# One decoder layer on one core: attention worked in pairs of heads, and a step with another order

## The chip, the cores and the metric

The kernel runs on one core of a Trainium2 chip. The metric is the device time of one execution in microseconds (us); three executions of the kernel before gave 1241.56, 1243.33 and 1244.72 us, so the median is 1243.33 us.

## The reference

One layer of a decoder for 256 tokens of width 1024, all in float32. Cut to what matters here:

```
proj = rmsnorm(x) @ w_in            # 1024 -> 5120: q, k, v for two mixers, two gates
# mixer 1, 8 heads of 64: stick-breaking attention
log_keep = where(causal, -softplus(z), 0);  tail = reverse_cumsum(log_keep) - log_keep
a = where(causal, exp(log_sigmoid(z) + tail), 0);  y = a @ v
# mixer 2, 8 heads of 64: softmax attention with a relative bias
y = softmax(where(causal, z + bias, -inf)) @ v
h = x + (sigmoid(g1) * (y_sb @ w_proj_sb) + sigmoid(g2) * (y_mb @ w_proj_moba)) @ w_out
h = h + moe(rmsnorm(h))             # top 4 of 32 experts, each 1024 -> 2 x 1024 -> 1024
out = rmsnorm(h)
```

`z` is the product of queries and keys, scaled by 1/8. The weights of the 32 experts are 12 MB each.

## The kernel before

The order of the work on each engine is written out by hand, one queue per engine, with semaphores between them. TensorE (PE) does first the projection in "units" (`unit(u)`, L849): a unit is 8 matmuls over the 8 slices of the depth, into `bank[u % 2]`, and ScalarE (ACT) copies it out (`evacuate`, L467). A "T" unit gives 128 columns of q or k, transposed (128 by 256), an "N" unit gives a 128 by 512 tile of values or gates. Ten units run ahead of attention, 18 are left as fill: one in each of the 16 steps of attention (`fill_at`), and two more in steps 3 and 6 (`second_at`).

Attention goes head by head, heads 0 to 7 stick-breaking, 8 to 15 softmax (called MoBA in the names). Three pieces on PE belong to a head. `scores(s)` (L866) multiplies the head's 64 rows of q and k: even heads lie in partitions 0 to 63, odd ones in 64 to 127, so a head uses one half of the rows of the array. `middle(s)` (L886) is the cumulative sum by two triangle matrices for a stick-breaking head (full array), and three transposes of the probabilities for a softmax head. `mix_values(s)` (L903) multiplies 128 rows by the head's 64 columns of values, so it uses one half of the columns. A float32 matmul stands in the trace as two instructions, called passes below. A step of the loop at L922 is: scores of head s, fill unit, middle of head s-1, second unit if there is one, values of head s-2.

Between scores and middle of a stick-breaking head stand Abs, Exp and Ln on ACT (L490, L495, L496), max and add on VectorE (DVE, L659) and the causal mask on GpSimd (POOL, L407). Between middle and values stand Exp on ACT (L512) and the mask (L407). For a softmax head DVE adds the bias and takes the maxima, ACT does Exp (L502), DVE scales (L666 to L674), and after the transposes ACT copies (L515). DVE copies the output of a pair of heads to `yT` (L680).

After attention come the projections of the mixers (L945), the merge with the gates, `w_out` (L956), the router, and then the loop over the experts, which reads all their weights through a ring of 12 slots of 1 MB. SyncE (SP) issues the load of a slot when PE has used what lay in it (L310 gate and up weights, L315 down weights). The weights of the mixers' projection, of `w_out` and of the first expert go into the same ring, each load when the last unit of the columns that lay there is done.

Of the kernel before, what the change touches and what calls it, by code (L numbers as in the profile page):

```python
# [46 lines left out]
def hybrid_layer(nc, x, norm_mix_g, w_in, w_proj_sb, w_proj_moba, w_out, rel_bias, norm_ffn_g,  # L47
# [31 lines left out]
    for s in range(NH):  # L79
        fill_at[s] = len(units)  # L80
        units.append(first_fill[s])
        if s in second_fill:
            second_at[s] = len(units)
            units.append(second_fill[s])
# [8 lines left out]
    with ctx:  # L93
# [6 lines left out]
        bank = [ctx.enter_context(nc.psum_tensor(f"bank{i}", [P, 512], F32)) for i in range(8)]  # L100

# [259 lines left out]
        def _(pool):  # L361
# [48 lines left out]
            for s in range(HSB + 1):  # L410
                if s < HSB:
                    pool.wait_ge(softplus, s + 1)
                    mask(att_s[:, s % 2, :], keep_rd)
                if s >= 1:
                    pool.wait_ge(weight_raw, s)
                    mask(att_w[:, (s - 1) % 2, :], weights_rd)
# [12 lines left out]
        def _(act):  # L429
# [56 lines left out]
            for s in range(NH + 1):  # L486
                if s < HSB:

                    act.wait_ge(z_ps, s + 1)
                    link(nc.scalar.activation(att_a[:, s % 2, :], bank[2 + s % 3][:, 0:TRI], ACT.Abs))  # L490
                    if s == 0:
                        act.wait_ge(u_out, 16)
                    if s >= 2:
                        act.wait_ge(softplus, s - 1)
                    link(nc.scalar.activation(att_e[:, s % 2, :], att_a[:, s % 2, :], ACT.Exp, scale=-1.0))  # L495
                    nc.scalar.activation(att_e[:, s % 2, :], att_e[:, s % 2, :], ACT.Ln, bias=1.0).then_inc(ln_rd, 1)  # L496
                elif s < NH:

                    b = s % 2
                    act.wait_ge(score_rd, s - HSB + 1)  # L500
                    for q, (c0, c1) in enumerate(((0, P), (P, TRI))):
                        nc.scalar.activation(att_s[:, b, c0:c1], att_s[:, b, c0:c1], ACT.Exp, bias=nmx[:, b, q:q + 1],  # L502
                                             accum_out=rs[:, b, q:q + 1]).then_inc(prob_raw, 1)
                if s < NH:
                    evacuate(fill_at[s])
                h = s - 1
                if h >= 0:
                    act.wait_ge(mid_ps, h + 1)
                    if h >= 2:
                        act.wait_ge(pv_ps, h - 1)  # L510
                    if h < HSB:
                        nc.scalar.activation(att_w[:, h % 2, :], bank[2 + h % 3][:, 0:TRI], ACT.Exp  # L512
                                             ).then_inc(weight_raw, 1)
                    else:
                        nc.scalar.activation(att_w[:, h % 2, :], bank[6][:, 0:TRI], ACT.Copy).then_inc(probT_rd, 1)  # L515
                if s in second_at:
                    evacuate(second_at[s])
# [5 lines left out]
            act.wait_ge(pv_ps, NH)  # L523
# [73 lines left out]
        def _(dve):  # L597
# [53 lines left out]
            for s in range(NH + 2):  # L651
                b = s % 2
                if s < HSB:
                    z = bank[2 + s % 3][:, 0:TRI]
                    dve.wait_ge(z_ps, s + 1)
                    dve.wait_ge(ln_rd, s + 1)
                    if s >= 2:
                        dve.wait_ge(mid_ps, s - 1)
                    V.scalar_tensor_tensor(out=att_s[:, b, :], in0=z, scalar=0.0, in1=att_e[:, b, :], op0=ALU.max,  # L659
                                           op1=ALU.add).then_inc(softplus, 1)  # L660
                elif s < NH:
                    h = s - HSB
                    z = bank[2 + s % 3]
                    dve.wait_ge(z_ps, s + 1)
                    dve.wait_ge(mid_ps, s - 1)
                    V.tensor_tensor(att_s[:, b, 0:P], z[:, 0:P], bias[:, h, P - 1::-1], ALU.add)  # L666
                    link(V.tensor_tensor(att_s[:, b, P:TRI], z[:, P:TRI], bias[:, h, ::-1], ALU.add))
                    V.reduce_max(mx[:, b, 0:1], att_s[:, b, 0:P], AX_X)
                    link(V.reduce_max(mx[:, b, 1:2], att_s[:, b, P:TRI], AX_X))
                    V.tensor_scalar(nmx[:, b, :], mx[:, b, :], -1.0, None, ALU.mult).then_inc(score_rd, 1)  # L670
                    dve.wait_ge(prob_raw, 2 * (h + 1))
                    link(V.reciprocal(rr[:, b, :], rs[:, b, :]))
                    for q, (c0, c1) in enumerate(((0, P), (P, TRI))):
                        V.tensor_scalar(att_s[:, b, c0:c1], att_s[:, b, c0:c1], rr[:, b, q:q + 1], None, ALU.mult  # L674
                                        ).then_inc(prob_rd, 1)
                h = s - 2
                if h >= 1 and h % 2 == 1:
                    pair = h // 2
                    dve.wait_ge(pv_ps, h + 1)
                    V.tensor_copy(yT[:, pair, :], bank[5 + 2 * (pair % 2)][:, 0:T]).then_inc(pv_rd, 1)  # L680
# [146 lines left out]
        def _(pe):  # L827
# [38 lines left out]
            def scores(s):  # L866
                z = bank[2 + s % 3]
                if s >= 3:
                    if s - 3 < HSB:
                        pe.wait_ge(weight_raw, s - 2)  # L870
                    else:
                        pe.wait_ge(score_rd, s - 3 - HSB + 1)
                h = s % HSB
                r0 = HEAD_DIM * (h % 2)
                q = qkT[r0:r0 + HEAD_DIM, (0 if s < HSB else 8) + h // 2, :]
                k = qkT[r0:r0 + HEAD_DIM, (4 if s < HSB else 12) + h // 2, :]
                pe.wait_ge(unit_rd, unit_no[("T", K_SB if s < HSB else K_MB, h // 2)] + 1)
                if s < HSB:
                    mm(z[:, 0:T], k[:, 0:P], q, start=True, stop=True)
                    ins = mm(z[:, T:TRI], k[:, P:T], q[:, P:T], start=False, stop=True, skip_group_check=True)  # L880
                else:
                    mm(z[:, 0:P], q[:, 0:P], k[:, 0:P], start=True, stop=True)
                    ins = mm(z[:, P:TRI], q[:, P:T], k, start=True, stop=True)
                ins.then_inc(z_ps, 1)

            def middle(s):  # L886
                if s < HSB:

                    z = bank[2 + s % 3]
                    a = att_s[:, s % 2, :]  # L890
                    pe.wait_ge(keep_rd, s + 1)
                    mm(z[:, 0:T], neg_tri[:, :], a[:, 0:T], start=False, stop=True, skip_group_check=True)
                    mm(z[:, P:T], neg_one[:, :], a[:, T:TRI], start=False, stop=True, skip_group_check=True)
                    ins = mm(z[:, T:TRI], neg_tri[:, :], a[:, T:TRI], start=False, stop=True, skip_group_check=True)
                else:
                    pe.wait_ge(prob_rd, 2 * (s - HSB + 1))
                    if s > HSB:
                        pe.wait_ge(probT_rd, s - HSB)
                    for i in range(3):
                        ins = tp(bank[6][:, i * P:(i + 1) * P], att_s[:, s % 2, i * P:(i + 1) * P], ident[:, :])  # L900
                ins.then_inc(mid_ps, 1)

            def mix_values(s):  # L903
                if s < HSB:
                    pe.wait_ge(weights_rd, s + 1)
                else:
                    pe.wait_ge(probT_rd, s - HSB + 1)
                pair = s // 2
                if s == 0 or s == HSB:
                    pe.wait_ge(unit_rd, unit_no[("N", V_SB if s == 0 else V_MB, 1)] + 1)  # L910
                if pair >= 2:
                    pe.wait_ge(pv_rd, pair - 1)
                r0 = HEAD_DIM * (s % 2)
                o = bank[5 + 2 * (pair % 2)][r0:r0 + HEAD_DIM, :]
                v = values[:, :, s * HEAD_DIM:(s + 1) * HEAD_DIM]
                w = att_w[:, s % 2, :]
                mm(o[:, 0:T], v[:, 0, :], w[:, 0:T], start=True, stop=True)  # L917
                mm(o[:, P:T], v[:, 1, :], w[:, T:TRI], start=False, stop=True, skip_group_check=True).then_inc(pv_ps, 1)

            for u in range(lead):  # L920
                unit(u)
            for s in range(NH + 2):  # L922
                if s < NH:
                    scores(s)
                    unit(fill_at[s])
# [194 lines left out]
```

## Time and profile before

| | |
|---|---|
| median of three executions | 1243.33 us |
| the profiled execution's own time | 1241.16 us |
| its span in the trace | 1239.3 us |
| PE busy (matmul) | 1121.8 us, 91% |
| DVE, ACT, POOL busy | 205.8, 167.0, 18.6 us |
| moved by DMA | 437.11 MB, 353 GB/s over the span |

The busy share is an average over stages with different limits: attention lies in the tenth of the span from 55 to 190 us, the experts' loop in the last 960 us. A matmul's duration in a row includes the drain of its pipeline, so the distance between the starts of two groups tells more than their durations.

### The profile page before, as it was taken

What the parts mean: (1) busy time and instruction counts of PE and PEld (TensorE: products, weight loads), DVE (VectorE), ACT (ScalarE), POOL (GpSimd) and SP (SyncE); (2) the same over time, 40 slices, a digit from 0 to 9 for tenths busy, and PEclk for the clock granted to TensorE, in tenths of its full rate; (3) what the DMA queues carried; (4) which work ended last, traced back from release to release, by engine and by line L of the source; (5) the groups of instructions that cost most, each with busy time, mean ns of one, the idle gap of its engine ahead of it and who ended that gap; (6) DMA issues with size and microseconds to landing.
All of it is one profiled execution on the core that took longest, in us unless ns stands there. A gap on an engine that the chain in (4) does not pass through costs nothing.

```text
span 1239.3 us, 15513 instructions
## 1 busy us (share of the span) xinstructions
PE 1121.8 (91%) x6044; PEld 444.4 (36%) x6044; DVE 205.8 (17%) x420; ACT 167.0 (13%) x326; POOL 18.6 (1%) x68
## 2 busy tenths in 40 slices
PE   7999999958999999999999999999999998898885
PEld 6676444433333332323333233333333332322321
DVE  1301222141112111111111111111111111111111
ACT  2274222140000000000000000000000000000002
POOL 1010000000000000000000000000000000000000
PEclk9999999978999999999999999999999999999998
DMA  9922123338999999999999999999999999999994
GB/s 334 386 75 109 51 111 140 135 136 333 407 417 418 418 417 418 418 417 418 418 419 418 417 418 418 418 417 418 417 418 417 417 417 417 417 418 418 417 418 194
DMA packets 86628, 437.11 MB, mean 353 GB/s; under 512 B 7704, under 2 KB 7760, under 8 KB 53744
## 3 DMA queue, kind: packets, MB, share of 16 engines
q1 hardware_dynamic: 84880, 434.19, 86.3%
q10 hardware_dynamic: 1424, 1.57, 0.5%
q0 software_dynamic: 304, 1.06, 0.2%
q8 instruction: 14, 0.23, 0.1%
q14 instruction: 6, 0.05, 0.0%
HBM read 435.74 MB, written 1.06 MB: 352 GB/s over the span
## 4 chain that ended last, share of the span: by engine, by line
SPq 47%; PE 37%; DMA 9%; issue 4%; DVE 2%; ACT 1%; DVEq 0%
SPq L315 26%; SPq L310 20%; PE bank L1019 10%; DMA ring<-in_w_gate_up_dram 7%; PE bank L862 7%; PE bank L859 5%; PE bank L1049 3%; PE bank L945 2%; PE bank L956 2%; DMA ring<-in_w_down_dram 2%; PE bank L1002 2%; PE bank L993 1%; PE bank L917 1%; PE bank L839 1%; PE bank L1038 0%
## 5 line engine op out<-in xcount | busy, mean ns | idle before, releaser
L1019 PE MATMUL bank<-ring,gates 128*64 128x512 f32 x2048 | 476.9, 604 | 18.2 <-DMA ring<-in_w_gate_up_dram 15.3
L1049 PE MATMUL bank<-ring,gates 128*64 128x512 f32 x1024 | 244.2, 603 | 60.0 <-DMA ring<-in_w_down_dram 59.9
L1019 PEld LDWEIGHTS bank<-ring,gates 128*64 128x64 f32 x2048 | 135.1, 137 | 276.9 <-issue 191.3
L771 DVE TENSOR_SCALAR gates<-bank 128x512 f32<-128x512 f32 x32 | 22.1, 691 | 790.2 <-PE bank L1019 790.2
L1049 PEld LDWEIGHTS bank<-ring,gates 128*64 128x64 f32 x1024 | 64.0, 136 | 238.8 <-DMA ring<-in_w_down_dram 152.8
L862 PE MATMUL bank<-ring,colsT 128*128 128x512 f32 x192 | 85.0, 597 | 0.0
L1002 PE MATMUL bank<-gates,scatter_w 64*128 64x512 f32 x256 | 63.6, 615 | 0.8 <-ACT gates L570 0.7
L566 ACT ACTIVATE gates<-gates 128x512 f32<-128x512 f32 x32 | 20.2, 630 | 296.6 <-DVE gates L771 296.6
L859 PE MATMUL bank<-colsT,ring 128*128 128x256 f32 x256 | 58.8, 388 | 0.0
L993 PEld LDWEIGHTS bank<-onehot,qkT 128*128 128x128 bf16 x1536 | 47.7, 99 | 27.9 <-issue 25.2
L570 ACT ACTIVATE gates<-bank 128x512 f32<-128x512 f32 x32 | 19.1, 597 | 260.9 <-PE bank L1049 260.9
L993 PE MATMUL bank<-onehot,qkT 128*128 128x64 bf16 x1536 | 51.5, 195 | 2.3 <-ACT qkT L551 2.3
L859 PEld LDWEIGHTS bank<-colsT,ring 128*128 128x128 f32 x256 | 48.9, 194 | 7.5
L862 PEld LDWEIGHTS bank<-ring,colsT 128*128 128x128 f32 x192 | 35.7, 190 | 43.4 <-issue 43.3
L1002 PEld LDWEIGHTS bank<-gates,scatter_w 64*128 64x128 f32 x256 | 22.0, 186 | 41.3 <-issue 39.4
L561 ACT ACTIVATE gates<-bank 128x512 f32<-128x512 f32 x32 | 19.1, 597 | 114.6 <-PE bank L1038 114.6
L555 ACT ACTIVATE stat<-stat 128x1 f32<-128x1 f32 x32 | 6.5, 203 | 206.6 <-PE bank L1032 206.6
L945 PE MATMUL bank<-ring,yT 128*128 128x512 f32 x64 | 27.7, 594 | 0.0
L956 PE MATMUL bank<-ring,colsT 128*128 128x512 f32 x64 | 27.6, 592 | 0.0
L1013 PE MATMUL bank<-bgu,expert_sel 96*64 96x512 bf16 x128 | 20.2, 394 | 3.6 <-DVE gates L756 3.6
L421 POOL COPY expert_sel<-expert_row 96x64 bf16 x32 | 7.4, 233 | 1037.5 <-PE bank L993 1037.5
L1038 PEld LDWEIGHTS bank<-ident,gates 128*128 128x128 f32 x128 | 13.5, 141 | 26.0 <-issue 26.0
(167 smaller groups left out, 500.3 us busy)
## 6 DMA issues: line engine op xcount, KB each, us to landing
ring<-in_w_gate_up_dram SPq DMA_DIRECT2D x256, 1024.0 KB, 20.6
ring<-in_w_down_dram SPq DMA_DIRECT2D x128, 1024.0 KB, 24.6
ring<-in_w_in_dram SPq DMA_DIRECT2D x10, 2048.0 KB, 18.7
ring<-in_w_out_dram SPq DMA_DIRECT2D x1, 4096.0 KB, 14.1
ring<-in_w_proj_sb_dram SPq DMA_DIRECT2D x1, 2048.0 KB, 7.6
ring<-in_w_proj_moba_dram SPq DMA_DIRECT2D x1, 2048.0 KB, 13.4
resid<-in_x_dram SPq DMA_DIRECT2D x2, 512.0 KB, 3.7
bias<-u_scratch POOLq DMA_DIRECT2D x1, 1024.0 KB, 12.4
```

Of the source, the lines that this page charges most:

```text
L310: sp.dma_start(ring[:, s, :], src).then_inc(slot_in[s], 16)
L315: sp.dma_start(dst, src).then_inc(slot_in[s], 16)
L566: nc.scalar.activation(sig_t, gate_t, ACT.Sigmoid, scale=SWIGLU_ALPHA).then_inc(sig_rd, 1)
L771: V.tensor_scalar(gate_t, bank[4][:, :], SWIGLU_LIMIT, None, ALU.min).then_inc(gate_rd, 1)
L859: ins = mm(bank[u % 2][:, 0:T], w[:, k, j * P:(j + 1) * P], colsT[:, k, :], start=k == 0, stop=k == KD - 1)
L862: ins = mm(bank[u % 2][:, :], colsT[:, k, j * P:(j + 1) * P], w[:, k, :], start=k == 0, stop=k == KD - 1)
L945: ins = mm(bank[n % 4][:, :], yT[:, 4 * m + k, t * P:(t + 1) * P], w[:, k, c * CH:(c + 1) * CH], start=k == 0, stop=k == 3)
L956: ins = mm(bank[2 * t + c][:, :], colsT[:, k, t * P:(t + 1) * P], wo_sb[:, k, c * CH:(c + 1) * CH], start=k == 0, stop=k == KD - 1)
L993: ins = mm(bank[7][:, k * SLOTS:(k + 1) * SLOTS], pieces[i][:, t, k * P:(k + 1) * P], onehot[:, t, :], start=n == 0, stop=n == 3 * NT - 1)
L1002: ins = mm(bank[2 * t + c][:, :], scatter_w[r, t, :], y_t[r, :], start=False, stop=True, skip_group_check=True)
L1019: ins = mm(bank[4 + i][SLOTS * c:SLOTS * (c + 1), :], xeT[:, k, :], ring[:, k, i * D + c * CH:i * D + (c + 1) * CH], start=False, stop=k = ...
L1049: ins = mm(bank[6][SLOTS * c:SLOTS * (c + 1), :], rows, ring[:, KD + s, j * D + c * CH:j * D + (c + 1) * CH], start=k == 0, stop=k == KD - 1)
```

## The change

Attention goes pair by pair: 8 steps with two heads each. `scores(p)` and `mix_values(p)` issue the matmuls of the two heads in turn: first part of head 0, first part of head 1, second part of head 0, second part of head 1; each head writes scores to its own bank of four (`z_bank`), and values go to the two halves of one bank (`o_bank`). A step is: middle of the pair before, scores of the pair, its two fill units, second unit if the pair has one, values of the pair before. The middle of the last pair stands after the loop, the values of the last pair behind the first output tile of the mixers' projection. ACT does a pair's activations by kind (Abs twice, Exp twice, Ln twice); DVE and POOL follow the pairs. Semaphores `z_ps`, `mid_ps` and `pv_ps` count pairs. The transposed probabilities go to the head's bank of scores.

```
-            for s in range(NH + 2):
-                if s < NH:
-                    scores(s)
+            for p in range(PAIRS):
+                if p >= 1:
+                    middle(p - 1)
+                scores(p)
+                for s in (2 * p, 2 * p + 1):
                     unit(fill_at[s])
-                if 1 <= s <= NH:
-                    middle(s - 1)
-                if s in second_at:
-                    unit(second_at[s])
-                if s >= 2:
-                    mix_values(s - 2)
+                for s in (2 * p, 2 * p + 1):
+                    if s in second_at:
+                        unit(second_at[s])
+                if p >= 1:
+                    mix_values(p - 1)
+            middle(PAIRS - 1)
...
+                        if n == 0:
+                            mix_values(PAIRS - 1)
...
+            def scores(p):
...
+                for part in range(2):
+                    for b in range(2):
+                        z = z_bank[(2 * p + b) % 4]
+                        r0 = HEAD_DIM * b
+                        q = qkT[r0:r0 + HEAD_DIM, (0 if sticks else 8) + j, :]
+                        k = qkT[r0:r0 + HEAD_DIM, (4 if sticks else 12) + j, :]
+                        if sticks:
+                            if part == 0:
+                                ins = mm(z[:, 0:T], k[:, 0:P], q, start=True, stop=True)
+                            else:
+                                ins = mm(z[:, T:TRI], k[:, P:T], q[:, P:T], start=False, stop=True, skip_group_check=True)
+                        else:
+                            if part == 0:
+                                ins = mm(z[:, 0:P], q[:, 0:P], k[:, 0:P], start=True, stop=True)
+                            else:
+                                ins = mm(z[:, P:TRI], q[:, P:T], k, start=True, stop=True)
+                ins.then_inc(z_ps, 1)
+            def mix_values(p):
...
+                for part in range(2):
+                    for b in range(2):
+                        s = 2 * p + b
+                        o = o_bank[p % 2][HEAD_DIM * b:HEAD_DIM * (b + 1), :]
...
+            for p in range(PAIRS + 1):
+                if p >= 1:
+                    act.wait_ge(mid_ps, p)
+                    if p >= 2:
+                        act.wait_ge(pv_ps, p - 1)
+                    for b in range(2):
+                        z = z_bank[(2 * (p - 1) + b) % 4][:, 0:TRI]
+                        if p - 1 < SB_PAIRS:
+                            nc.scalar.activation(att_w[:, b, :], z, ACT.Exp).then_inc(weight_raw, 1)
+                        else:
+                            nc.scalar.activation(att_w[:, b, :], z, ACT.Copy).then_inc(probT_rd, 1)
+                if p < SB_PAIRS:
+
+                    act.wait_ge(z_ps, p + 1)
+                    absd = [mark(nc.scalar.activation(att_a[:, b, :], z_bank[(2 * p + b) % 4][:, 0:TRI], ACT.Abs))
+                            for b in range(2)]
...
+                    for b in range(2):
+                        act.wait_ge(act_step, absd[b])
+                        small.append(mark(nc.scalar.activation(att_e[:, b, :], att_a[:, b, :], ACT.Exp, scale=-1.0)))
+                    for b in range(2):
+                        act.wait_ge(act_step, small[b])
+                        nc.scalar.activation(att_e[:, b, :], att_e[:, b, :], ACT.Ln, bias=1.0).then_inc(ln_rd, 1)
...
+                if p < PAIRS:
+                    evacuate(fill_at[2 * p])
+                    evacuate(fill_at[2 * p + 1])
```

The two second units stay with heads 3 and 6, that is with pairs 1 and 3, behind both fill units of the pair. The wait for the weights of the mixers' projection stands once, ahead of its loop.

## Rows read from the trace of the kernel before

**Rows 1.** The page's part 4: the chain that ended last, by engine.
```profile
SPq 47%; PE 37%; DMA 9%; issue 4%; DVE 2%; ACT 1%; DVEq 0%
```

**Rows 2.** Windows: stretch, length, busy time of each engine, granted clock, DMA share, GB/s.
```profile
55.01:190.45 135.44, 135.40 (x489) 80.91 (x489) 24.36 (x79) 59.19 (x109) 6.50 (x16) 1.00 0.28 103
...
278.50:400.00 121.50, 117.90 (x740) 43.67 (x738) 20.02 (x37) 9.23 (x20) 1.16 (x5) 0.96 0.96 392
400.00:1239.00 839.00, 747.63 (x4398) 249.25 (x4394) 119.78 (x226) 68.28 (x147) 6.05 (x26) 0.99 1.00 410
```

**Rows 3.** Waits of SyncE's queue: who waited for whom, us in total, times, longest.
```profile
SPq L310 <- PE bank L1019: 93.9, 36, 30.4
```

**Rows 4.** Timeline of PE, step of a stick-breaking head: start, us, instruction.
```profile
83.29 0.65 PE L917 MATMUL bank<-att_w,values 128*64 128x256 f32 x2
...
84.08 0.70 PE L879 MATMUL bank<-qkT 64*128 64x256 f32 x2
84.62 0.38 PE L880 MATMUL bank<-qkT 64*128 64x128 f32 x2
84.93 3.72 PE L859 MATMUL bank<-colsT,ring 128*128 128x256 f32 x16
88.48 0.59 PE L892 MATMUL bank<-att_s,neg_tri 128*128 128x256 f32 x2
...
89.45 0.65 PE L917 MATMUL bank<-att_w,values 128*64 128x256 f32 x2
```

**Rows 5.** Timeline of PE, step of a softmax head.
```profile
134.24 0.48 PE L882 MATMUL bank<-qkT 64*128 64x128 f32 x2
...
135.09 7.13 PE L862 MATMUL bank<-ring,colsT 128*128 128x512 f32 x16
142.06 0.49 PE L900 MATMUL bank<-ident,att_s 128*128 128x128 f32 x3
142.48 0.65 PE L917 MATMUL bank<-att_w,values 128*64 128x256 f32 x2
```

**Rows 6.** Timeline of PE, end of attention: values of heads 14 and 15.
```profile
189.00 0.65 PE L917 MATMUL bank<-att_w,values 128*64 128x256 f32 x2
189.49 0.38 PE L918 MATMUL bank<-att_w,values 128*64 128x128 f32 x2
189.66 0.65 PE L917 MATMUL bank<-att_w,values 128*64 128x256 f32 x2
...
190.45 27.73 PE L945 MATMUL bank<-ring,yT 128*128 128x512 f32 x64
```

**Rows 7.** Timeline of PE, experts' loop: matmuls in turn on two halves.
```profile
310.37 3.65 PE L1019 MATMUL bank<-ring,gates 128*64 128x512 f32 x16
...
329.78 1.99 PE L1002 MATMUL bank<-gates,scatter_w 64*128 64x512 f32 x8
331.69 0.44 PE L1032 MATMUL bank<-ident,onehot_g 128*128 128x128 f32 x2
```

**Rows 8.** Timelines of ACT, then DVE and POOL: one stick-breaking head.
```profile
85.03 0.49 ACT L490 ACTIVATE att_a<-bank 128x384 f32<-128x384 f32 x1 [1.04 <-PE bank L880]
85.56 0.52 ACT L495 ACTIVATE att_e<-att_a 128x384 f32<-128x384 f32 x1
86.10 1.28 ACT L496 ACT_TABLE_LOAD   x1
87.39 0.52 ACT L496 ACTIVATE att_e<-att_e 128x384 f32<-128x384 f32 x1
...
89.09 1.28 ACT L512 ACT_TABLE_LOAD   x1
90.38 0.49 ACT L512 ACTIVATE att_w<-bank 128x384 f32<-128x384 f32 x1
...
88.00 0.56 DVE L659 SCALAR_TENSOR_TENSOR att_s<-bank,att_e 128x384 f32<-128x384 f32 x1 [3.39 <-ACT att_e L496]
...
88.63 0.41 POOL L407 TENSOR_SCALAR_AFFINE_SELECT att_s<-att_s 128x256 f32<-128x256 f32 x1 [10.32 <-DVE att_s L659]
```

More of the change, by code:

```diff
@@ L78, in hybrid_layer @@
     fill_at, second_at = {}, {}
[L79 to L84, printed above, removed]
+    for p in range(NH // 2):
+        for s in (2 * p, 2 * p + 1):
+            fill_at[s] = len(units)
+            units.append(first_fill[s])
+        for s in (2 * p, 2 * p + 1):
+            if s in second_fill:
+                second_at[s] = len(units)
+                units.append(second_fill[s])
     unit_no = {u: n for n, u in enumerate(units)}
@@ L100, in hybrid_layer @@
         bank = [ctx.enter_context(nc.psum_tensor(f"bank{i}", [P, 512], F32)) for i in range(8)]
+        z_bank = [bank[2], bank[3], bank[4], bank[7]]
+        o_bank = [bank[5], bank[6]]
+        PAIRS = NH // 2
+        SB_PAIRS = HSB // 2
         ring = sb("ring", [P, RING, SLOT])
@@ L408, in mask @@
                                         pattern=[[0, 2], [1, P]], channel_multiplier=-1).then_inc(ready, 1)
[L410 to L416, printed above, removed]
+            for p in range(SB_PAIRS + 1):
+                for b in range(2):
+                    if p >= 1:
+                        pool.wait_ge(weight_raw, 2 * (p - 1) + b + 1)
+                        mask(att_w[:, b, :], weights_rd)
+                for b in range(2):
+                    if p < SB_PAIRS:
+                        pool.wait_ge(softplus, 2 * p + b + 1)
+                        mask(att_s[:, b, :], keep_rd)
             def experts(done):
@@ L650, in _ @@
             dve.wait_ge(bias_in, 16)
-            for s in range(NH + 2):
[L652 to L680, printed above, removed]
@@ L886, in middle @@
[L886 to L901, printed above, removed]
@@ L903, in mix_values @@
[L903 to L918, printed above, removed]
+            def scores(p):
+                sticks = p < SB_PAIRS
+                j = p % SB_PAIRS
+                if p == 1:
+                    pe.wait_ge(u_rd, 1)
+                if p >= 2:
+                    if p - 2 < SB_PAIRS:
+                        pe.wait_ge(weight_raw, 2 * (p - 1))
+                    else:
+                        pe.wait_ge(probT_rd, 2 * (p - 1 - SB_PAIRS))
+                pe.wait_ge(unit_rd, unit_no[("T", K_SB if sticks else K_MB, j)] + 1)
+                for part in range(2):
+                    for b in range(2):
+                        z = z_bank[(2 * p + b) % 4]
+                        r0 = HEAD_DIM * b
[12 more added lines that the diff above has]
+                ins.then_inc(z_ps, 1)
@@ new lines, in middle @@
+            def middle(p):
+                for b in range(2):
+                    z = z_bank[(2 * p + b) % 4]
+                    a = att_s[:, b, :]
+                    if p < SB_PAIRS:
+                        pe.wait_ge(keep_rd, 2 * p + b + 1)
+                        mm(z[:, 0:T], neg_tri[:, :], a[:, 0:T], start=False, stop=True, skip_group_check=True)
+                        mm(z[:, P:T], neg_one[:, :], a[:, T:TRI], start=False, stop=True, skip_group_check=True)
+                        ins = mm(z[:, T:TRI], neg_tri[:, :], a[:, T:TRI], start=False, stop=True, skip_group_check=True)
+                    else:
+                        pe.wait_ge(prob_rd, 2 * (2 * (p - SB_PAIRS) + b + 1))
+                        for i in range(3):
+                            ins = tp(z[:, i * P:(i + 1) * P], a[:, i * P:(i + 1) * P], ident[:, :])
+                ins.then_inc(mid_ps, 1)
@@ new lines, in mix_values @@
+            def mix_values(p):
+                if p < SB_PAIRS:
+                    pe.wait_ge(weights_rd, 2 * (p + 1))
+                else:
+                    pe.wait_ge(probT_rd, 2 * (p - SB_PAIRS + 1))
+                if p == 0 or p == SB_PAIRS:
+                    pe.wait_ge(unit_rd, unit_no[("N", V_SB if p == 0 else V_MB, 1)] + 1)
+                if p >= 2:
+                    pe.wait_ge(pv_rd, p - 1)
+                for part in range(2):
+                    for b in range(2):
+                        s = 2 * p + b
+                        o = o_bank[p % 2][HEAD_DIM * b:HEAD_DIM * (b + 1), :]
+                        v = values[:, :, s * HEAD_DIM:(s + 1) * HEAD_DIM]
+                        w = att_w[:, b, :]
+                        if part == 0:
+                            ins = mm(o[:, 0:T], v[:, 0, :], w[:, 0:T], start=True, stop=True)
+                        else:
+                            ins = mm(o[:, P:T], v[:, 1, :], w[:, T:TRI], start=False, stop=True, skip_group_check=True)
+                ins.then_inc(pv_ps, 1)
```

103 lines of the change are left out of this document (54 added, 49 removed).

## The prediction

> **What bounds the kernel now.** I read the chain of waits first, then the windows by stage, then the queue waits of SyncE, and last the timelines of the attention stage. The chain is SyncE's queue for 47% and PE for 37% [rows 1]: for most of the span the transfers of expert weights set the pace, yet each transfer is started by PE. The windows show where one gives way to the other [rows 2]. From 400 us on DMA is busy at share 1.00; from 278.5 to 400 it is at 0.96 while PE works through the full ring. So from about 278.5 us a nearly unbroken stream of weights runs to the end, and SyncE's largest wait is for PE to use up slots [rows 3]. The stream begins when PE reaches the first expert; all later work has its distance from that moment. What comes off the path before it should come off the end one for one.
>
> Attention is such a path. From 55.01 to 190.45 us PE is busy 135.40 of 135.44 us at granted clock 1.00, while ACT has 59 us, DVE 24 us and DMA a share of 0.28 [rows 2]. The reader should see that PE waits for nobody here: only fewer or shorter PE pieces, or a new wait of PE, can change this stage.
>
> **What the pieces cost now**, from start to start. A stick-breaking head: values 84.08-83.29 = 0.79 us, scores 84.93-84.08 = 0.85, middle 89.45-88.48 = 0.97 [rows 4]. A softmax head: scores 135.09-134.24 = 0.85, middle 142.48-142.06 = 0.42 [rows 5], values as before. A "T" unit is 88.48-84.93 = 3.55 [rows 4], an "N" unit 142.06-135.09 = 6.97 [rows 5]. Check: 8 x (0.79+0.85+0.97) + 8 x (0.79+0.85+0.42) + 8 x 3.55 + 10 x 6.97 = 20.9+16.5+28.4+69.7 = 135.5, against 135.44 measured.
>
> The unit gives the length of a pass: 6.97/16 = 0.436 us for 512 columns, 0.109 per 128. A head's scores and its values each are two passes of 256 columns and two of 128, so 6 x 0.109 = 0.65 us; the rest, 0.20 for scores and 0.14 for values, is fixed cost at changes of the tile (for instance 84.62-84.08 = 0.54 where two passes of 256 make 0.44 [rows 4]). The middle has 8 x 0.109 = 0.87, fixed 0.10; the transposes 0.33, fixed 0.09.
>
> **What matmuls in turn on two halves cost.** The trace has both kinds of halves. On halves of the rows, 8 passes of 512 columns (four matmuls, halves in turn) take 331.69-329.78 = 1.91 us, where one after another they would take 8 x 0.436 = 3.49 [rows 7]. That is 4.4 pass lengths: the second pass of one matmul runs beside the first pass of the next, in the other half, and the first and last passes stand alone, (8+1)/2 = 4.5. On halves of the columns 16 passes take 3.65 us, 8.4 lengths [rows 7]; the same picture. And at the end of attention, where two heads' values stand side by side, head 15 starts 189.66-189.49 = 0.17 us after head 14's last matmul, which is one pass of 128 and not two [rows 6].
>
> I apply that pattern to a pair, in lengths of 128 columns. Head 0's two passes of 256, then head 1's, then the two of 128 each: head 0 from 0 to 4; head 1 from 2 to 6; head 0's second part 4 to 6, beside head 1; head 1's second part, in order behind it, 6 to 8. So 8 lengths against 12. Softmax scores have the short part first, and again come to 8. The pair costs 8 x 0.109 = 0.87 us plus one fixed part: scores 1.07 against 1.70, a gain of 0.63; values 0.87+0.14 = 1.01 against 1.58, a gain of 0.57. Two middles in a row save one fixed part, 0.10 (0.09 for transposes).
>
> *Bounds.* At best the second head costs nothing: gains of 0.85 and 0.79 a pair. At worst nothing runs side by side and each turn adds 0.10 (the excess at 84.62): three turns make scores 2.0 us, a loss of 0.3, and values come out even. I take the middle value since the two rows of [rows 7] are the same construction at both kinds of halves, only with longer passes.
>
> **Sum.** 8 x (0.63+0.57+0.10) = 10.4 us. The units are unchanged in number and kind. Moving the last values behind the first projection tile costs nothing by itself: they are PE work either way. It hides ACT's two copies, about 1.0 us (2 x 0.49, by the Exp of the same shape at 90.38 [rows 8]), behind 8 passes of 512, 3.5 us. In the kernel before the last heads' overlap (0.14) and a small pause there cancel.
>
> **New waits, and what covers them.** The middle now heads the step, so everything on PE stands behind it if the mask is late. From the end of a pair's scores: 0.10 to ACT's start, Abs twice 0.98, a table load 1.28 (only in the first pair; later the Exp of the weights has loaded it), Exp twice 1.04, table load 1.28, Ln 0.52, then 0.09 to DVE, 0.56, 0.07 to POOL, 0.41 [rows 8]: 6.3 us for the first head of the first pair, 6.8 for the second, which PE needs 0.87 later. PE is busy meanwhile with two T units, 7.1 us. The margin is 0.8 us, the thinnest of the change. For pair 2 the chain is 5.0 us and the cover 7.1+1.0; its ACT work before, two Exp of 0.49, hides behind the scores' 1.07. Pairs 1 and 3 have one N unit more. The table load for the weights' Exp runs before the middle ends (89.09, where the middle ends at 89.45 [rows 4, 8]); in the new order ACT issues it after copying out the last unit, 0.4+1.3 us, while the middle alone gives PE 1.8. If that cover fails by something, it delays ACT, not PE. ACT spares about two table loads per pair; it waits anyway, so that is worth nothing by itself, but it is why the pair's chain fits. In the softmax half a head's chain fitted behind one N unit with no gap on PE [rows 5]; a pair has two such units for twice the work. SyncE's loads: the values' weights are done later than before relative to the k units, so w_proj's second half starts later by one unit or less, with the eight N units of the softmax half, 8 x 6.97 = 56 us, still ahead of its use; the other loads move with PE.
>
> **A rule on each side.** One that speaks against this change: the Trainium skill, "TensorEngine Tiling (Array Packing)", Key Properties, says that changing the tiling mode drains the engine, while changing the tile within a mode does not. By that rule the fixed part is paid once per group and not per turn, and the sum stays as above; the 0.10 between 84.08 and 84.93 for two weights on the same half would be something else. Another would give more: the Trainium skill, "TensorE: Matmul & The Clock Gate", Part 3 (Packing small matmuls), puts the span of packed matmuls at one duration plus about 4 ns per tile. This would make the second head free, the best bound above; [rows 7] disagree in part, 1.91 us where that rule has 1.75.
>
> **Result.** The profiled span goes from 1239.3 to 1228.9, that execution's time from 1241.16 to 1230.8. It lies 2.2 us under the median of the runs shown, so the median goes to 1243.33-10.4 = 1232.9 us.
>
> **Rivals.**
> *The second head is free.* The pair costs what a head costs: 8 x (0.85+0.79+0.10) = 13.9 us, time 1229.4. For it: passes of two halves could be held ready further ahead when short. Against: the 4.4 lengths where 4 would be full overlap [rows 7]. Chance 0.18.
> *Halves in turn do not overlap at this size.* With passes of 128 and 256 columns the weight loads and changes of tile take the gain: scores between even and 0.3 worse, values even, middles 0.1 better: about 8 x 0.1 = 0.8, time 1242.5. For it: fixed parts of 0.14 to 0.20 beside 0.65 of columns. Against: 0.17 at 189.66 [rows 6]. Chance 0.10.
> *The gain does not reach the end.* If the weights' stream were bound to something other than PE's arrival at the first expert, 1243. Against: SyncE's waits [rows 3] and PE's dense 278.5 to 400. Chance 0.03.
> *Slower: a wait at the first middle that lowers the clock.* The mask of pair 0 is late by more than the 0.8 us margin, PE stops at the head of step 1, and the granted clock drops as it did in the stretch up to 400 us, at 0.96 [rows 2]; at 1.2 GHz each us of PE work costs one more. It decides once the wait plus the work at the low level exceeds 10.4 us: with 3 us of wait and 11 at the low level the loss is 14, time 1243.33-10.4+14 = 1247. For it: the thin margin and three engines in the chain. Against: even a chain longer by a whole table load would stop PE for only 0.5 us, and only pairs 0 and 2 lack the cover of an N unit. Chance 0.04.
>
> **Chances.** The forecast holds 0.65. A difference under 0.3% (3.7 us) cannot be told from none. Forecast and free second head are faster by more than that: with a share of the intermediate cases, faster 0.85, within 0.3% 0.10, slower 0.05. The likeliest case's own range is 1230 to 1236 (the execution-to-execution spread is 1.5 us each way). The range over the cases goes from the free second head less 1 us, 1228.5, to a gain of 3, 1240.
>
> **What would show it.** PE from end of lead units to the first w_proj matmul: 55.0 to 179.1 (10.4 less, and the last pair's values of 1.0 now behind it); a scores group from 1.0 to 1.1 us, values about 1.0; no PE wait at middle; first expert matmul near 268 us; DMA without gaps from there to the end, at about 410 GB/s as before [rows 2]. Wrong if the pairs take over 1.5 us, if PE waits for POOL at a middle, or if attention shrinks by 10 and the span does not.

## The result, and the profile after

The changed kernel takes 1231.74 us (median of 4, 1230.13 to 1232.23), the kernel before, run beside it, 1243.82: ratio 0.9901, 95% interval 0.9886 to 0.9916, a gain of 12.1 us where 10.4 was forecast. The profiled execution took 1230.13 us with a span of 1228.1, 11.2 less than before.

The page's parts 1 and 4 of the changed kernel, to be read beside [rows 1]:

```profile
PE 1110.8 (90%) x6044; PEld 436.0 (36%) x6044; DVE 204.9 (17%) x420; ACT 154.9 (13%) x318; POOL 18.5 (2%) x68
...
SPq 55%; PE 34%; issue 4%; DMA 4%; DVE 2%; ACT 1%; DVEq 0%
```

The same 6044 matmuls; ScalarE has 8 instructions less, all of them table loads, 8 x 1.28 = 10.3 of the 12.1 us that its busy time fell by. The windows of the changed kernel, by the same columns as [rows 2]: attention up to the first projection matmul, from there to the first product of the first expert, and the two stretches of the experts:

```profile
53.75:174.81 121.06, 121.06 (x482) 71.96 (x481) 23.22 (x79) 45.33 (x98) 6.40 (x16) 1.00 0.32 117
174.81:267.19 92.38, 77.45 (x253) 37.10 (x251) 27.98 (x62) 22.72 (x33) 0.23 (x1) 0.88 0.35 136
267.19:389.00 121.81, 118.21 (x743) 43.98 (x744) 20.32 (x39) 9.23 (x20) 1.16 (x5) 0.97 0.96 392
389.00:1228.00 839.00, 747.52 (x4396) 249.03 (x4392) 119.63 (x225) 68.28 (x147) 6.05 (x26) 1.00 1.00 409
```

and the stretch of the kernel before that answers to the second line:

```profile
190.45:277.52 87.07, 72.14 (x242) 35.17 (x241) 27.87 (x62) 21.02 (x31) 0.23 (x1) 0.92 0.35 140
```

The 11.2 us between the two profiled executions come from four places, not one:

| stage | before | after | difference |
|---|---|---|---|
| start to first scores | 55.01 | 53.75 | -1.26 |
| attention, with the last pair's values (0.80) | 135.44 | 121.86 | -13.58 |
| projections to first expert, without them | 87.07 | 91.58 | +4.51 |
| experts to the end | 961.78 | 960.91 | -0.87 |

Attention gave 3.2 us more than forecast, and the stretch behind it took 4.5 us longer. In it the granted clock reads 0.88 where it read 0.92. Most of this third row cannot be put down to the change: executions of one and the same kernel differ by some 3 us, and the profiled one of the kernel before (granted clock 0.987 as the mean of the execution, 0.984 in the changed kernel's) is of the rarer kind (see "What was missing" below). The timeline of PE in the changed kernel shows where the time goes:

```profile
238.43 3.68 PE L863 MATMUL bank<-ident,scaled 128*128 128x128 f32 x16 [4.05 <-DVE scaled L638]
...
260.06 7.19 PE L1120 MATMUL bank<-bias,yT 32*128 32x512 f32 x8
...
268.04 10.56 PE L1059 MATMUL bank<-ring,gates 128*64 128x512 f32 x40
```

and the same instructions of the kernel before:

```profile
253.17 3.19 PE L839 MATMUL bank<-ident,scaled 128*128 128x128 f32 x16 [4.05 <-DVE scaled L615]
...
273.62 3.97 PE L1080 MATMUL bank<-bias,yT 32*128 32x512 f32 x8
```

The eight bias products need 7.19 us instead of 3.97: they run wholly at the lower level, 1.2 GHz. The waits around them (4.05 us and three of 2.3 to 3.6) are the same in both kernels within 0.1 us; what differs is which work the low level catches. By starts, 3.2 of the 4.5 us are in the bias products, and 1.2 in the transposes and router products ahead of them.

The pieces of attention, timeline of PE in the changed kernel, beside [rows 4, 5]:

```profile
78.29 0.65 PE L951 MATMUL bank<-att_w,values 128*64 128x256 f32 x4
78.77 0.39 PE L953 MATMUL bank<-att_w,values 128*64 128x128 f32 x4
79.09 0.70 PE L926 MATMUL bank<-att_s,neg_tri 128*128 128x256 f32 x2
...
81.04 0.70 PE L909 MATMUL bank<-qkT 64*128 64x256 f32 x4
81.58 0.39 PE L911 MATMUL bank<-qkT 64*128 64x128 f32 x4
81.89 7.17 PE L883 MATMUL bank<-colsT,ring 128*128 128x256 f32 x32
...
124.92 0.88 PE L932 MATMUL bank<-ident,att_s 128*128 128x128 f32 x6
125.72 0.49 PE L914 MATMUL bank<-qkT 64*128 64x128 f32 x4
```

Read starts: a pair's values 79.09-78.29 = 0.80, a pair's scores 81.89-81.04 = 0.85. That is one head's price before (0.79 and 0.85), within a hundredth. The count at the ends of the lines doubled (x4 for x2) and the time did not. Two middles in a row cost 81.04-79.09 = 1.95, as much as twice 0.97 before.

### The profile page after: what moved, and what is told of

Read it like the earlier page. It is cut to its first block, busy times and chain, and to the rows that moved or that the text cites. A ratio compares the mean times of both kernels' runs of the same rounds, so it can differ in the third digit from the quotient of the medians.

```text
span 1228.1 us, 15468 instructions
## 1 busy us (share of the span) xinstructions
PE 1110.8 (90%) x6044; PEld 436.0 (36%) x6044; DVE 204.9 (17%) x420; ACT 154.9 (13%) x318; POOL 18.5 (2%) x68
## 4 chain that ended last, share of the span: by engine, by line
SPq 55%; PE 34%; issue 4%; DMA 4%; DVE 2%; ACT 1%; DVEq 0%
SPq L322 30%; SPq L317 24%; PE bank L1059 8%; PE bank L886 7%; PE bank L883 5%; PE bank L1089 3%; PE bank L983 2%; PE bank L996 2%; DMA ring<-in_w_down_dram 2%; DMA ring<-in_w_gate_up_dram 1%; PE bank L1042 1%; PE bank L1033 1%; PE bank L863 1%; PE bank L1120 1%; SPq L338 0%
## 5 line engine op out<-in xcount | busy, mean ns | idle before, releaser
L799 DVE TENSOR_TENSOR gates<-gates 128x512 f32<-128x512 f32 x32 | 22.2, 693 | 3.1
```

The source lines that it names most:

```text
L799: V.tensor_tensor(sig_t, sig_t, gate_t, ALU.mult).then_inc(pass_step, 1)
```

## Experiments

All start from the changed kernel unless said otherwise. "Attention" is first scores to first projection matmul in the profile (121.06 in the changed kernel).

**1 to 3. Turns undone**: the loops over heads and parts are swapped, so that a pair's matmuls come head after head; for scores, for values, and for both.

```
-                for part in range(2):
-                    for b in range(2):
+                for b in range(2):
+                    for part in range(2):
```

> Changed kernel (median 1231.7 us, span 1228.1), only the scores of a pair are issued head after head instead of in turn. Theory 1, the second head runs wholly beside the first when issued in turn: a scores group is 0.85 us in the changed kernel and becomes 1.56 to 1.70 here (0.14 less than two heads where the second one's first pass may slip in), attention grows by 5.7 to 6.8 us, time 1237.4 to 1238.5. Theory 2, the pattern of my prediction (one pass in two stands alone): growth 8 x 0.63 = 5.0 us, time 1236.7. Theory 3, the gain comes from the new order of the step and fewer groups, not from turns: under 1 us, time 1232.

> Changed kernel, only the values of a pair are issued head after head. Theory 1: the group goes from 0.80 us to 1.45 (two heads of 0.79 less the 0.14 of overlap seen in the kernel before where two heads' values stood side by side), attention grows by 8 x 0.65 = 5.2 us, time 1236.9; with no such overlap 6.3 us, 1238.0. Theory 2: 8 x 0.57 = 4.6 less 1.1 for that overlap, 3.5 us, 1235.2. Theory 3: under 1 us, time 1232.

> Changed kernel with scores and values both head after head: what is left is the order of the step, pairs on all engines and ACT's batches by kind. Theory 1: the two costs add, 10.9 to 13.1 us, time 1242.6 to 1244.8, no better than the kernel before by more than 1.5 us. Theory 3: stays at 1232 to 1234, since order is what pays.

Measured: 1231.39, 1231.00 and 1231.57 us, ratios to before 0.9891, 0.9891 and 0.9899. Attention 121.10, 121.10 and 121.15 us. Neither theory on the turns' price (1 and 2) holds; turns are worth nothing. PE's timeline of the kernel with both undone:

```profile
78.74 0.66 PE L951 MATMUL bank<-att_w,values 128*64 128x256 f32 x4
79.22 0.40 PE L953 MATMUL bank<-att_w,values 128*64 128x128 f32 x4
79.55 0.70 PE L926 MATMUL bank<-att_s,neg_tri 128*128 128x256 f32 x2
...
81.50 0.71 PE L909 MATMUL bank<-qkT 64*128 64x256 f32 x4
82.04 0.39 PE L911 MATMUL bank<-qkT 64*128 64x128 f32 x4
82.36 7.17 PE L883 MATMUL bank<-colsT,ring 128*128 128x256 f32 x32
```

Scores 0.86, values 0.81. Although head 1's matmuls were issued after all of head 0's, the first parts of both heads still form one group of four in time (L909 x4, then L911 x4), and so do the second parts: both heads run at once. The same timeline, asked for no more than 81.45 to 81.60 us, has the first pass of both heads already started, over half a us ahead of head 0's second part:

```profile
81.50 0.49 PE L909 MATMUL bank<-qkT 64*128 64x256 f32 x2
```

So either being neighbours in the queue is enough, or the gain was in the order and in the pairs of the other engines. Run 10 decides.

**4. ScalarE head by head**: Abs, Exp, Ln of one head, then of the other.

```
+                    for b in range(2):
+                        link(nc.scalar.activation(att_a[:, b, :], z_bank[(2 * p + b) % 4][:, 0:TRI], ACT.Abs))
+                        link(nc.scalar.activation(att_e[:, b, :], att_a[:, b, :], ACT.Exp, scale=-1.0))
+                        nc.scalar.activation(att_e[:, b, :], att_e[:, b, :], ACT.Ln, bias=1.0).then_inc(ln_rd, 1)
```

> Changed kernel, ScalarE does Abs, Exp, Ln of head 0 and then of head 1, so two more table loads of 1.28 us stand in each stick-breaking pair's chain. Theory 1, TensorE waits only if the chain is longer than its cover: first pair, second head's mask 0.1 + 2 x (0.49+1.28+0.52+1.28+0.52) + 1.13 = 9.4 us after the scores, needed at 7.1 + 0.87 = 8.0, so one wait of about 1.4 us at the second head of the first middle; pair 2 about 8.1 against 9.0, no wait; attention grows by 1.4 us, time 1233. Rival: a wait there lowers the granted clock and costs more, 1236 and up. Rival: batches are what makes the change pay, each pair waits, 8 us more.

Measured: 1230.71 us. Timeline of PE:

```profile
64.71 0.70 PE L921 MATMUL bank<-att_s,neg_tri 128*128 128x256 f32 x2 [1.39 <-POOL att_s L414]
...
74.10 7.11 PE L881 MATMUL bank<-ring,colsT 128*128 128x512 f32 x16 [0.28 <-ACT qkT L491]
```

The wait at the first pair is 1.39 us for the 1.4 worked out, and attention grows by 2.7 (178.18-54.42 = 123.76), with an extra wait of 0.28 that I had not foreseen, at 74.10 and again at 102.91: a fill unit's bank was copied out late. Yet the median is not longer. In the profiled execution the stretch to the first expert took 266.15-178.18 = 87.97 instead of 92.38; the low level caught less work. The mean granted clock of the four executions tells why the median hides the loss: three read 0.986 and took 1229.91 to 1231.11 us, the fourth read 0.983 and took 1233.04, while the four of the changed kernel, all at 0.984, took 1230.13 to 1232.23. Times of executions with unlike clocks do not show 2 or 3 us of one stage.

**5. Values of the last pair directly behind its middle**

```
             middle(PAIRS - 1)
+            mix_values(PAIRS - 1)
...
-                        if n == 0:
-                            mix_values(PAIRS - 1)
```

> Changed kernel, the last pair's values stand right behind its middle instead of behind the first projection tile. Theory: TensorE waits for ScalarE's two copies, 0.1 + 0.39 + 0.49, and then for VectorE to copy nothing that the first tile needs: attention grows by 1.0 us, time 1232.7, which timed runs may hardly tell from 1231.7; the profile must show a gap of about 1 us ahead of the values. Rival: the place is worth nothing, no gap.

Measured 1232.21 us, not to be told from 1231.74. In the timeline of PE the wait stands as expected:

```profile
176.60 0.65 PE L951 MATMUL bank<-att_w,values 128*64 128x256 f32 x4 [0.96 <-ACT att_w L510]
```

**6. Attention padded to its old length**

```
+            pe.wait_ge(pv_rd, 7)
+            extra(31, 5)          # 31 matmuls of 128x256 into a free bank
             pe.wait_ge(proj_in, 16 * 2)
```

> Changed kernel with 31 added matmuls of 128x256 (each about 0.44 us, 13.6 us in all, results unused) between the middle of the last pair and the mixers' projection, so that this stage takes as long as before. Theory, whatever comes off or on before the experts passes to the end one for one: 1231.7 + 13.6 = 1245.3 (the kernel before is at 1243.8; the difference would be that the changed kernel loses more at the low clock between 234 and 270 us). If the stage's lower clock depends on when it starts, the pad may change that loss by up to 4 us either way. Rival, the end is bound to the weights' stream from an earlier time: under 1238.

Measured 1243.63 us (10 runs), ratio to before 0.9994, interval 0.9984 to 1.0005. The pad took 189.51-176.12 = 13.39 us, and with it the time of the kernel before is back. So the length of this stage is what sets the gain. The profiled execution, like that of the kernel before, has a mean clock of 0.987, and both read 0.83, 0.70 and 0.67 from 250 to 280 us. That looks as if the end of the stage set what the low level catches, but run 10, whose stage ends within 0.3 us of this one's, has the other pattern. The windows from 250 us of this kernel:

```profile
250.00:260.00 10.00, 6.87 (x32) 4.48 (x32) 4.64 (x9) 6.15 (x10) 0.00 (x0) 0.83 0.98 395
260.00:270.00 10.00, 1.52 (x11) 0.54 (x9) 8.86 (x27) 4.30 (x8) 0.00 (x0) 0.70 0.06 25
270.00:280.00 10.00, 9.14 (x66) 5.10 (x68) 0.89 (x2) 2.29 (x3) 0.23 (x1) 0.67 0.01 2
```

and the changed kernel's:

```profile
250.00:260.00 10.00, 3.50 (x55) 2.90 (x55) 5.68 (x16) 3.66 (x4) 0.00 (x0) 0.56 0.00 0
260.00:270.00 10.00, 10.00 (x21) 3.60 (x20) 0.89 (x2) 0.00 (x0) 0.23 (x1) 0.50 0.00 0
```

**7 and 8. TensorE kept busy in the waits of the router's stretch**, in the changed kernel and in the one before:

```
+            extra(8, 7)
             pe.wait_ge(scaled_rd, 4)
...
+            extra(6, 3)
             pe.wait_ge(routed, 1)
...
+            extra(7, 3)
             pe.wait_ge(weighted, 1)
...
+            extra(4, 3)
             pe.wait_ge(piece_rd, 3)
```

> Changed kernel with 25 added matmuls of 128x256 (results unused) in TensorE's waits between the output projection and the first expert: 8 in the wait of 4.05 us, 6 in that of 2.96, 7 in 3.59, 4 in 2.26. Theory, the stretch from 234 to 268 us lost about 4.5 us more at granted clock 0.5 to 0.8 than in the kernel before, and 7 to 9 us in all: with TensorE kept busy the clock stays at 1.00, the router, the bias products (7.19 us) and the first gate products run at full speed: 6 us less, time 1225.5. Rival, the waits are on VectorE and ScalarE's chain and the added matmuls delay what they stand before: no gain or up to 3 us slower. Rival, the clock falls anyway: 1232 to 1234.

> Kernel before with the same 25 added matmuls. Theory: with the clock kept up in both, the difference between this run and that of the changed kernel with them is attention alone, 13.6 us, instead of the 12.1 measured; so this kernel is at 1225.5 + 13.6 = 1239.1. Rival: the difference stays at 12.1 or falls to 10.4.

Measured: 1224.49 and 1236.30 us, ratios 0.983 (0.9812 to 0.9847) and 0.9938 (0.9922 to 0.9955). Each kernel gains 7 to 8 us, so the low level did cost both. Whether their distance grows to 13.6 us cannot be told: the medians are 11.8 apart, but the four executions of each spread over 4.7 and 3.7 us, and the shortest of each are 14.2 apart. The kernel before came through to 292 us at full clock in its profile, the changed one still fell to the low level from 260 to 267 us (clock 0.52 there).

**9. The pauses closed further**: 9, 7, 8 and 5 matmuls in place of 8, 6, 7 and 4, and 7 ahead of the second expert.

> Changed kernel with 36 added matmuls (results unused) in TensorE's waits: 9, 7, 8 and 5 in the four waits between the output projection and the first expert, 7 ahead of the second expert. With 25 of them the time was 1224.5 and the low clock level still stood at 260 to 267 us and 284 to 288. Theory, the remaining pauses of 0.5 us and the one of 3.6 let the clock fall: with both filled it stays up through 300 us, the first gate products take 8.8 instead of 10.9 us, 2 to 4 us less, 1221 to 1222.5. Rival, from 268 us on the weights' stream sets the pace, so only the part before the first slot is freed counts: 1223 to 1224.5. Rival, the added work delays the router chain: slower than 1224.5.

Measured 1221.19 us (1219.83 to 1221.79), ratio 0.982, interval 0.9805 to 0.9835: the fastest version. From the timeline of PE and the windows of this kernel:

```profile
256.23 3.70 PE L1128 MATMUL bank<-bias,yT 32*128 32x512 f32 x8
...
260.31 8.75 PE L1067 MATMUL bank<-ring,gates 128*64 128x512 f32 x40
```

```profile
250.00:260.00 10.00, 9.84 (x80) 6.36 (x80) 4.14 (x16) 3.66 (x4) 0.23 (x1) 1.00 0.01 2
260.00:270.00 10.00, 10.00 (x79) 3.83 (x76) 0.00 (x0) 0.00 (x0) 0.00 (x0) 1.00 0.68 247
```

The clock is at 1.00 in both windows, the bias products are back at 3.70, and the first expert starts at 259.85 instead of 267.19.

**10. Heads never side by side.** Pairs on all engines stay; on TensorE full-array work stands between the heads:

```
+                if p >= 1:
+                    middle(p - 1, (0,))
+                scores(p, (0,))
+                if p >= 1:
+                    middle(p - 1, (1,))
+                scores(p, (1,))
+                unit(fill_at[2 * p])
+                if p >= 1:
+                    mix_values(p - 1, (0,))
+                unit(fill_at[2 * p + 1])
...
+                if p >= 1:
+                    mix_values(p - 1, (1,))
```

> Changed kernel with the same pairs on all engines, but on TensorE the two heads of a pair never stand side by side: middle head 0, scores head 0, middle head 1, scores head 1, fill unit, values head 0 of the pair before, fill unit, values head 1 (first scores and last values stay together). Issuing heads in turn proved to be worth nothing; theory now, the second head is free because its matmuls stand in the queue right behind the first one's, in the other half of the array: with full-array work between them each head costs what it cost before, attention grows by 7 x (0.85 + 0.80) + 7 x 0.1 for more changes of tile = 12.3 us, from 124.9 to 137 us, time 1241 to 1245. Rival, the engine finds the second head's matmuls over other work too: no growth, 1232. Rival, pairs on the other engines (fewer waits and table loads) are what pays: no growth, 1232.

Measured 1245.26 us (10 runs), ratio 1.0011, interval 1.0002 to 1.0021: all of the gain is gone. Attention 189.80-54.72 = 135.08 us. Timeline of PE:

```profile
94.02 0.65 PE L953 MATMUL bank<-att_w,values 128*64 128x256 f32 x2
...
94.81 0.70 PE L927 MATMUL bank<-att_s,neg_tri 128*128 128x256 f32 x2
...
97.81 0.70 PE L909 MATMUL bank<-qkT 64*128 64x256 f32 x2
98.34 0.38 PE L911 MATMUL bank<-qkT 64*128 64x128 f32 x2
98.65 3.72 PE L883 MATMUL bank<-colsT,ring 128*128 128x256 f32 x16
```

Groups of two, 0.79 and 0.84 us a head, as before the change. It grew by 14.0, not 12.3: the pieces change more often between full and half array, and the middle of one head, for instance, takes 1.08 us (94.81 to the next scores at 95.89) instead of 0.97. Together with runs 1 to 3 this shows the cause: what pays is that the two halves' matmuls are neighbours in TensorE's queue. Pairs on the other engines pay nothing by themselves.

This run also answers run 6. From first projection matmul to first expert, in this kernel and in run 6:

```profile
189.80:281.20 91.40, 76.06 (x251) 36.62 (x249) 27.86 (x62) 22.72 (x33) 0.23 (x1) 0.88 0.35 139
```

```profile
189.51:277.54 88.03, 73.14 (x251) 35.38 (x249) 27.86 (x62) 16.86 (x28) 0.23 (x1) 0.92 0.25 97
```

The same work begins 0.3 us apart, yet one takes 3.4 us longer at clock 0.88. The moment at which the stretch begins does not decide this by itself.

**11. The middle in its old place**, between the two fill units.

```
-                if p >= 1:
-                    middle(p - 1)
                 scores(p)
-                for s in (2 * p, 2 * p + 1):
-                    unit(fill_at[s])
+                unit(fill_at[2 * p])
+                if p >= 1:
+                    middle(p - 1)
+                unit(fill_at[2 * p + 1])
```

> Changed kernel with the step ordered as in the kernel before: scores of the pair, first fill unit, middle of the pair before, second fill unit, second unit, values. Theory, the order is worth little beyond its covers: ScalarE starts a pair's chain 3.6 us later, and copies out a fill unit later, so TensorE waits some 1 to 2 us for that copy in pair 2, attention grows by 1 to 3 us, time 1232 to 1235. Rival, the order carries the gain: 1240 and up.

Measured 1230.97 us. Attention 179.26-55.27 = 123.99, 2.9 more than in the changed kernel. In PE's timeline it waits twice for a fill unit's bank to be copied out:

```profile
74.71 7.10 PE L886 MATMUL bank<-ring,colsT 128*128 128x512 f32 x16 [1.70 <-ACT qkT L491]
...
104.63 7.11 PE L886 MATMUL bank<-ring,colsT 128*128 128x512 f32 x16 [1.70 <-ACT qkT L491]
```

They stand at pairs 1 and 3, before the extra unit, and not at pair 2 as I had expected: it is the extra unit, third of its step, that wants the bank of the step's first. The order of the change is thus worth 2.9 us of attention. The median does not show it, as in run 4: three of the four executions read a clock of 0.986 or 0.988, and the fourth, at 0.984 like those of the changed kernel, took 1234.38 us, 2.6 more than their median.

## Why the prediction was right, and where it was not

*The path.* That PE alone bounds attention, and that what comes off there comes off the end, held: run 6 puts the time back by padding that stage. "One for one" holds within a microsecond where executions with the same clock are compared, see below.

*The pair's price.* This term of the sum was mis-sized: scores 1.07 were 0.85, values 1.01 were 0.80, so 8 x (0.85+0.78) = 13.0 us came off where I had 9.6. The misreading can be named. I took the 4.4 lengths of [rows 7] for a pattern in which the first and last passes stand alone, 4.5. But a group on half arrays has a fixed part of 0.14 to 0.20 us, which I had worked out one paragraph earlier, and 4 x 0.436 + 0.17 = 1.91 fits. My pattern with its fixed part would have been 4.5 x 0.436 + 0.17 = 2.13. The group on column halves spoke against me too: I took 3.65, a duration with the drain in it, but the next group of that timeline starts at 313.95,

```profile
313.95 1.57 PE L993 MATMUL bank<-onehot,qkT 128*128 128x64 bf16 x48
```

so it took 3.58 us, against 8 x 0.436 + 0.14 = 3.63 with nothing alone and 8.5 x 0.436 + 0.14 = 3.85 by my pattern. The kernel before even shows the first passes themselves. Its timeline asked for 329.7 to 330.2 us only, before the next pass starts at 330.31, has two started, not one:

```profile
329.78 0.70 PE L1002 MATMUL bank<-gates,scatter_w 64*128 64x512 f32 x2
```

For short passes the two readings lie at 1.07 and 0.85 us, and 0.85 was measured. The Trainium skill, "TensorE: Matmul & The Clock Gate", Part 3 (Packing small matmuls), has one duration plus about 4 ns per tile; this case agrees, 0.85 for 0.85 and 0.80 for 0.79. The same part of the Trainium skill's page has matmuls start and end strictly in program order. Run 3 differs: there head 1's first part starts at 81.50 with head 0's, 0.54 us ahead of head 0's second part, which was issued before it. The measurement decides, and it fits that turns are not needed.

*The row at 189.66.* [rows 6] were no evidence of a limit of the array. Head 15's values waited for ScalarE's copy, in the timeline of ACT before:

```profile
189.11 0.49 ACT L515 ACTIVATE att_w<-bank 128x384 f32<-128x384 f32 x1 [0.70 <-PE bank L900]
```

It ends at 189.60, and the matmul starts at 189.66. A start that I read as the engine's pace was a semaphore's.

*The middles.* I had 0.10 saved per pair; stick-breaking heads save nothing (1.95 against 1.94), transposes 0.04 (0.80 against 0.84). With the 13.0 above this makes 13.2 of the 13.6 us; the last 0.4 is not taken apart.

*The covers.* No wait arose in attention: PE is busy for all of its 121.06 us. The margin of 0.8 us was measured: in POOL's timeline the two masks of the first pair start at 60.45,

```profile
60.45 0.86 POOL L414 TENSOR_SCALAR_AFFINE_SELECT att_s<-att_s 128x256 f32<-128x256 f32 x2 [37.74 <-DVE att_s L681]
```

the first (0.41) ends at 60.86, and PE reaches it at 61.62, 0.76 later. The same sum gave run 4's wait to 0.01 us.

*What was missing.* The forecast lay within 1.2 us of the median although its main term was 3.4 us too small. My first rival, the free second head with 1229.4 us, is what happened in attention. That the median still lies so near is in part luck: of the 0.8 us that I had for the middles only 0.2 came, and 12.1 us is the low side of the gain, as the next paragraphs show. The sign that I gave, the first gate product near 268 us, came true (268.04), but by differences that cancel: 3.2 us more from attention and 1.3 at the start, against 4.5 from the clock.

The clock's part I had priced only as the result of a new wait. It needs none: the old waits of the router's stretch suffice. And it varies between executions of one kernel, which I did not look at. For 35 executions of the kernel before, run beside the experiments, the mean granted clock is known, and they fall into two kinds:

| mean granted clock | kernel before | changed kernel and runs 1 to 3, all with attention of 121.1 us |
|---|---|---|
| 0.986 or 0.987 | 7: 1241.01 to 1242.51 us | 2: 1227.52 and 1229.14 us |
| 0.983 to 0.985 | 28: 1243.55 to 1245.49, median 1244.62 | 14: 1230.13 to 1233.39, median 1231.6 |

In the lower row, with the clock alike, the gain is 13.0 us: nearly all of attention's 13.6 reaches the end. The profiles show where the difference lies. From first projection matmul to first expert, without the last pair's values, it is 87.07 us in the kernel before and 87.2 or 87.3 in runs 4, 6 and 11, all four at 0.986 to 0.988; it is 91.58 in the changed kernel and 90.6 to 91.7 in runs 1, 2, 3, 5 and 10, all at 0.984 or 0.985. So most of the 4.5 us of the table come from which executions were profiled, and the 12.1 us of the result may be a little low: the four executions of the kernel before that stood beside it had a median of 1243.82, where 15 later ones had 1244.46.

What decides between the two kinds is not shown. Runs 4 and 11, with attention near 124 us, were at 0.986 or more in 6 of 8 executions, the changed kernel and runs 1 to 3 in 2 of 16, so what stands before the stretch may change the chances; runs 6 and 10 show that it does not settle them.

The 1.3 us at the start are nothing that the change did. The work is the same in both kernels; the PE timelines of the kernel before and of the changed one have its first 128 matmuls as

```profile
12.32 29.02 PE L859 MATMUL bank<-colsT,ring 128*128 128x256 f32 x128
```

```profile
12.30 27.79 PE L883 MATMUL bank<-colsT,ring 128*128 128x256 f32 x128
```

and over the runs, whose code is the same up to there, this group takes 27.79 to 29.08 us.

## What to carry to other kernels

Put matmuls that use different halves of the array next to each other in TensorE's queue, in whatever order among themselves, and with nothing of the full array between them: the second then costs nothing, and 16 heads saved 13 us. Before working out a pattern from a group's length, take the fixed cost of entering and leaving it off, and look whether a start was set by a semaphore. And where TensorE has waits of 2 to 4 us ahead of a stage, read the granted clock in both kernels: such a stretch gives or takes several us for reasons that have nothing to do with the change, even between two executions of one kernel. Compare stages only between profiles whose clock reads alike. Here 36 unused matmuls in those waits were worth another 10.5 us.

## What the runs showed of the hardware

- Two heads' matmuls in the other halves run wholly side by side when issued head after head, 0.86 us for scores against 0.85 in turn.
- The clock's loss in the waits' stretch comes in two sizes for the same work: from first projection matmul to first expert 92.38 us in the changed kernel, 91.40, 92.47 and 92.43 in runs 1 to 3 and 91.40 in run 10, but 88.03, 87.97 and 88.11 in runs 6, 4 and 11. Executions of one kernel differ accordingly: the kernel before has none of its 35 between 1242.51 and 1243.55 us.
- Matmuls in different halves need not start in the order of issue: in run 3 head 1's first part starts 0.54 us before head 0's second.
- Unused matmuls of 0.44 us in TensorE's waits raised the granted clock there to 1.00 and shortened the kernel from 1231.7 to 1221.2 us, without delaying the router's chain: from one wait's end to the next it is 254.52-250.64 = 3.88 us in the changed kernel and 252.06-248.17 = 3.89 in run 9.
